# Splitting GpSimd's weight subtraction into pieces of two blocks, in a two-layer transformer kernel

## What is computed

```python
n = rms_norm(h, norm_mix_w[layer])
h = h + token_mixer(n, positions, w_in[layer], ...)
n = rms_norm(h, norm_ffn_w[layer])
h = h + conv_gated_mlp(n, w_ffn_in[layer], ...)
...
x = x + g1 * mix_lat
x = x + g2 * _sq_relu_mlp(_modulate(_rmsnorm(x, norm2_g[layer]), sh2, sc2), w_mlp1[layer], w_mlp2[layer])
```

## Time and profile before

| | before |
|---|---|
| median of three executions | 3695.28 us |
| the profiled execution: its time | 3697.86 us |
| its span, from first to last instruction | 3696.1 us |
| mean granted clock of TensorE | 0.952 |
| TensorE busy | 3334.1 us, 90% |
| VectorE busy | 2352.3 us, 64% |
| ScalarE busy | 1555.8 us, 42% |
| GpSimd busy | 1424.0 us, 39% |

### The profile page before, as it was taken

One profiled execution on the slowest core, in us unless ns is written; L12 is line 12 of the kernel. 1 busy time (PEld: TensorE's weight loads), 2 busy tenths in 40 slices (PEclk: granted clock), 3 DMA queues, 4 the chain that ended last, 5 costly groups with the idle time before them and its releaser, 6 DMA issues.

```text
span 3696.1 us, 58768 instructions
## 1 busy us (share of the span) xinstructions
PE 3334.1 (90%) x21604; PEld 2999.2 (81%) x21604; DVE 2352.3 (64%) x3370; ACT 1555.8 (42%) x2196; POOL 1424.0 (39%) x672
## 2 busy tenths in 40 slices
PE   5898989899989999999987987888887999999998
PEld 4888988898867878878865977888886788888886
DVE  5777777776746873883874766676765653535353
ACT  4344433443334443443434554354443443434343
POOL 2334443444323444444421333444442344444442
PEclk7999999999989999999998998899998999999999
DMA  4655555555565556556543756554564566666653
GB/s 159 203 188 185 192 188 189 179 192 191 173 219 181 182 173 186 182 172 186 175 151 120 252 167 197 190 189 157 182 205 170 190 194 189 186 185 186 188 183 108
DMA packets 262387, 672.95 MB, mean 182 GB/s; under 512 B 28263, under 2 KB 66888, under 8 KB 261448
## 3 DMA queue, kind: packets, MB, share of 16 engines
q1 hardware_dynamic: 262152, 669.81, 56.4%
HBM read 663.38 MB, written 6.32 MB: 181 GB/s over the span
## 4 chain that ended last, share of the span: by engine, by line
PE 56%; DVE 21%; issue 12%; ACT 5%; POOL 3%; DMA 2%; DVEq 1%; SPq 0%; ACTq 0%; POOLq 0%
PE psum L639 21%; PE psum L640 10%; PE psum L632 4%; PE psum L634 4%; PE psum L633 4%; POOL w_lo L497 3%; ACT w_hi L487 2%; PE psum L709 2%; DVE w_lo L497 2%; DVE psum L478 2%; PE psum L637 1%; DVE work L1262 1%; PE psum L1406 1%; DVE work L763 1%; DVE work L1641 1%
## 5 line engine op out<-in xcount | busy, mean ns | idle before, releaser
L497 POOL TENSOR_TENSOR w_lo<-raw,w_hi 128x1024 fp32r<-128x1024 f32 (+3 forms) x668 | 1423.8, 2133 | 2240.6 <-ACT w_hi L487 2239.3
L487 ACT ACTIVATE w_hi<-raw 128x1024 fp32r<-128x1024 f32 (+3 forms) x1112 | 1045.8, 947 | 1353.2 <-PE psum L634 616.7
L632 PE MATMUL psum<-act_a,w_lo 128*128 128x256 f32 x3072 | 923.3, 301 | 32.5 <-DVE w_lo L497 13.6
L497 DVE TENSOR_TENSOR w_lo<-raw,w_hi 128x1024 fp32r<-128x1024 f32 (+3 forms) x444 | 538.9, 1214 | 580.9 <-ACT w_hi L487 572.7
L633 PE MATMUL psum<-act_a,w_hi 128*128 128x256 f32 x3072 | 886.1, 288 | 0.0
L634 PE MATMUL psum<-act_a,w_hi 128*128 128x256 f32 x3072 | 885.4, 288 | 0.0
L639 PE MATMUL psum<-act_a,w_hi 128*128 128x512 f32 x2295 | 828.1, 402 | 26.7 <-DVE act_a L751 10.8
L639 PE MATMUL psum<-act_b,w_hi 128*128 128x512 f32 x2096 | 760.9, 404 | 29.7 <-DVE act_b L1649 17.7
L640 PE MATMUL psum<-act_a,w_lo 128*128 128x256 f32 x2295 | 647.3, 282 | 0.0
L632 PEld LDWEIGHTS psum<-act_a,w_lo 128*128 128x128 f32 x3072 | 608.2, 198 | 42.4 <-issue 18.5
L633 PEld LDWEIGHTS psum<-act_a,w_hi 128*128 128x128 f32 x3072 | 608.1, 198 | 3.1 <-issue 1.9
(11 more groups left out here) (335 smaller groups left out, 3348.4 us busy)
## 6 DMA issues: line engine op xcount, KB each, us to landing
raw<-w_mlp SPq DMA_DIRECT2D x256, 512.0 KB, 4.3
raw<-w_up SPq DMA_DIRECT2D x176, 512.0 KB, 3.7
raw<-w_dil SPq DMA_DIRECT2D x192, 384.0 KB, 3.4
work<-w_ada SPq DMA_DIRECT2D x288, 256.0 KB, 4.0
raw<-w_hg SPq DMA_DIRECT2D x128, 320.0 KB, 3.1
raw<-w_delta SPq DMA_DIRECT2D x64, 512.0 KB, 4.1
raw<-w_out SPq DMA_DIRECT2D x64, 512.0 KB, 5.7
raw<-w_down SPq DMA_DIRECT2D x64, 512.0 KB, 3.8
```

Of the source, the lines that this page charges most:

```text
L487: act.activation(w_hi[:, t % SPLIT, 0:nb * P], raw[:, t % RAW, 0:nb * P], ACT.Copy)\
L497: eng.tensor_tensor(w_lo[:, t % SPLIT, 0:nb * P], raw[:, t % RAW, 0:nb * P], w_hi[:, t % SPLIT, 0:nb * P], ALU.subtract)\
L632: pe.matmul(bank[:, 0:S], wl, src[:, kt, 0:S], start=first, stop=False)
```

## The change

GpSimd makes the low part in pieces of two blocks (256 columns): an item of eight blocks takes four instructions in place of one, an item of six takes three, an item of five takes three (of 256, 256 and 128 columns), an item of two blocks one as before. Only the last piece raises the semaphore, only the first is preceded by the wait, and the pieces stand back to back in GpSimd's stream. VectorE's items stay whole (`step = nb`).

```diff
                 nb = ph.items[t][1]
                 wait(eng, "hi_ready", i * ph.ipb + (ph.g0 + t + 1))
-                eng.tensor_tensor(w_lo[:, t % SPLIT, 0:nb * P], raw[:, t % RAW, 0:nb * P],
-                                  w_hi[:, t % SPLIT, 0:nb * P], ALU.subtract)\
-                   .then_inc(sem(f"lo_ready_{who}"), 1)
+                step = 2 if who == "pool" else nb
+                for b in range(0, nb, step):
+                    cols = slice(b * P, min(b + step, nb) * P)
+                    ins = eng.tensor_tensor(w_lo[:, t % SPLIT, cols], raw[:, t % RAW, cols],
+                                            w_hi[:, t % SPLIT, cols], ALU.subtract)
+                ins.then_inc(sem(f"lo_ready_{who}"), 1)
```

## The result

The changed kernel takes 3607.84 us (median of four, 3598.61 to 3613.75), the kernel before beside it 3696.03 us (median of four). The ratio is 0.976, with a 95% interval of 0.9743 to 0.9777: 88 us faster. The forecast was 3652 us, 43 us faster. The side was right and the time lies in the range, but the gain is twice the size that was forecast.

What follows compares the result with a forecast made beforehand. TensorE was taken to wait mostly for VectorE, held during single GpSimd instructions. Gains 23.5 ("one") + 17.6 + 4 ("two") + 3.6 ("up") + 3 ("out", "ctx"), less 4 and 5, made 43 us: 3695 to 3652 us, range 3605 to 3698.

Steps and rivals of the forecast that it cites:

- Rival 3: VectorE isn't let in between pieces and is held for the whole item: slower, 3726 us; chance 0.06.
- (f): Phase "two", wait at L2082: L2011 and L2012 held for shorter, 2.2 us, eight times, 17.6 us gained.
- (g): Phase "two", scans (L1994) ahead of L2011 and L2012: fewer hits, 0.5 us a body, 4 us gained.
- (a): Phase "one", wait at L1432: L1486 done some 1.2 us sooner, the wait goes, 5.6 us counted.
- (e): Phase "one", wait at L1396: L1310 gains, but L1316 and L1320 give it back; 0.2 us, eight times, 1.6 us.
- (d): Phase "one", wait at L1384: L783 and L785 hit by two subtractions; 0.8 us, eight times, 6.4 us gained.
- rival 2: Shorter waits keep the clock at 2.4 GHz in "two", sometimes "one": some 25 us more, 3627 us; chance 0.08.
- (h): Phase "two", wait at L2212: a train pays every piece once; nothing, between 1 us lost and 1 gained a body.
- (b): Phase "one", wait at L1571: L785 released sooner, 0.6 us, six times, 3.6 us gained.
- (c): Phase "one", wait at L1597: one hit on L1262 shortened, 0.9 us, seven times, 6.3 us gained.
- Rival 1: VectorE operations let in early are followed by others held by further pieces; about 5 us left, 3690 us; chance 0.16.
- Rival 4: GpSimd falls behind in "two": 2 us a body come back, gain in "one" stays, 3675 us; chance 0.05.

Runs made afterwards that it cites:

- long-first kernel: Against the kernel before: GpSimd's items cut into as many instructions as in the change, the long piece first, then pieces of two columns; 3693.86 us, ratio 0.9992.

## Why the prediction was right in kind and wrong in size

**The mechanism** stands. L2011 and L2012 went from 2.29 and 2.28 us to 1.22 and 1.21, where the forecast had them done 2.2 us sooner together; it was 2.1. Rival 3, that VectorE isn't let in between pieces without a wait between them, is out: four pieces ran back to back there. That operations with an operand in PSUM aren't held is borne out too: in the kernel before, no group of VectorE's operations that read PSUM, line by line and shape by shape, has a longest duration over 4% above its median. The Trainium skill (SBUF — State Buffer, section "Who interferes with whom") says that a VectorE instruction with two SBUF inputs and a GpSimd instruction that reads SBUF exclude each other for the whole instruction, whichever starts first; the traces agree, with the old L1641 at up to 2514 ns beside whole items and 846 ns beside pieces of 256 columns, in place of 424, and with GpSimd's long piece at 2.25 us in place of 1.82 where VectorE was first. The Trainium skill's warning (GPSIMD Engine Reference, section 2.1) that one instruction's end doesn't hold back the next was no obstacle to the hand-over.

**Step (f)** was right: L2011 and L2012 give 2.1 us a body, and the wait at L2082 fell by 19.3 us, against 17.6 for (f) and 4 for (g), the scans ahead of it, of which some 2 came. **Step (a)** was right: 6.4 us against 5.6. **Step (e)** was nearly right: the wait at L1396 grew by 1.6 us where a gain of 1.6 was counted. **Step (d)** was too high: 3.2 us at L1384 against 6.4.

**Four steps made the forecast too low.** The first is the largest.

1. *The pairs "up" and "down"*, 3.6 us in the sum, measured 21 us alone. Two things were missed. The waits at the ends of "up" fell by 8.0 us, not 3.6. Before, L1649 alone was held for 2.2, 2.2 and 1.7 us ahead of the three ends, and TensorE's waits fell by 3.0, 3.2 and 1.8 us, so at the first two more than this one hold came off. In the changed kernel VectorE has no work left over there: it pauses for 0.78 us or more before its L688, which it didn't before. And the last "down" gave 11.0 us, for which the sum had no term.
2. *The clock*, nothing in the sum (rival 2 placed some 25 us of it in "two"). TensorE's busy time fell from 3334.1 to 3310.2 us with the same 21604 products, 24 us. But "two" has only 3.2 us of it, and its granted clock stays at 0.90 to 0.91: 4.6 us of the wait at L2082 are left in nearly every body, and in the 2 us behind one of them (2289 to 2291) the clock is 0.50, as before. The most is in the last "down", 7.9 us; out has 3.1, "one" 2.7, and the rest is in smaller parts. The last section says what is known of it.
3. *The losses*, 9 us in the sum: 4 for late low parts, 5 for new hits. Late low parts cost 1.6 us (TensorE's waits for GpSimd went from 12.9 us, of which the forecast had read only the 7.5 at L639, to 14.5), and of TensorE's waits for VectorE the one at L1396 grew by 1.6 us and no other by as much. So some 3 us of the 9 can be seen. New hits that only made a gain smaller can't be told apart in these traces, and the long-first kernel doesn't settle it, since its unchanged time is a sum of gains and losses of about this size.
4. *Trains*, step (h), nothing in the sum, measured 8.0 us (32.4 to 24.4). The forecast let each piece of 0.77 us hold a train for 0.77 us. The traces show the price to be smaller. Before, with whole items:

```profile
2380.87 3.50 DVE L2141 TENSOR_SCALAR work<-work 128x256 f32<-128x256 f32 x3
2384.40 2.59 DVE L2146 SCALAR_TENSOR_TENSOR work<-work 128x255 f32<-128x255 f32 x6
```

After, at the same place:

```profile
2313.50 1.96 DVE L2144 TENSOR_SCALAR work<-work 128x256 f32<-128x256 f32 x3
2315.49 4.16 DVE L2149 SCALAR_TENSOR_TENSOR work<-work 128x255 f32<-128x255 f32 x6
```

The first three win 1.54 us, and the six behind them, none of which was held before, lose 1.57. So the train does take it back, as the forecast said of this place; but from the first line's start to the last one's end it is 6.12 us before and 6.15 after, with nine pieces of GpSimd beside it in place of three whole items, so the added fixed time of GpSimd's costs the train nothing. Five of the nine pieces fall beside the six L2149 and add 1.57 us to them, 0.31 us each: less than a piece's own 0.77. TensorE's wait behind this train is 0.75 us shorter (3.39 before, 2.64 after). The operation ahead of the train gives 0.41 of it (the copy at L2136, 0.88 us before, 0.47 after); where the rest comes from wasn't followed. In "one" steps (b) and (c) were too low, 7.7 us at L1571 against 3.6 and 10.3 at L1597 against 6.3; with (a), (d) and (e) the five waits give 26.0 us against 23.5, and TensorE's shorter busy time the other 2.7 of the 28.6.

Together, by the kernels with one phase changed: 17 us more than forecast in the pairs, with their share of the clock, 7 in "one", 7 in "two", 5 in out, ctx and out2, and the 9 that the sum took off for losses, since what the phases gained is already net of them. These make the 45 that were missing. That the time still lies in the range, 3 us above its lower end, is luck: the range reached so far down for rival 2, the clock in "two", and that is not what happened.

**Rival 1** (trains take it back) is out as the rule, though L1396 and L2141 to L2150 show it at two places. **Rival 4** (GpSimd late in "two") is out for two blocks; with pieces of one block its waits were 27.9 us and still worth it.

## What to carry to other kernels

When an operation on VectorE has the same shape and place each time and its longest duration is several times its median, look at what GpSimd has under way at that moment: the hold shows as a longer duration, not as a wait. What it costs is set by the length of one GpSimd instruction, so cut GpSimd's elementwise work into pieces as short as its slack allows; cutting VectorE's as well gained nothing here. A delay of GpSimd's long instructions by about a microsecond or less gave 32 us in this kernel, whose bodies repeat, so a single timing doesn't prove a cause: vary the length, and put the long piece first. Time taken off VectorE pays only where TensorE waits for it: half of its subtractions in "one" moved away, and it brought nothing.

## What was not expected of the hardware

A wait of TensorE of under 2 us can go with a fall of the clock, but its length doesn't decide it. Before, in the last "down", L1821 is held, TensorE waits 1.83 us and its next four products take 3.53 us:

```profile
1904.42 2.19 DVE L1821 TENSOR_TENSOR work<-work 128x512 f32<-128x512 f32 x1
```

```profile
1906.67 3.53 PE L1893 MATMUL psum<-work 64*128 64x512 f32 x4 [1.83 <-DVE work L1821]
```

After, it is held for one piece, TensorE waits 0.74 us and the same four products take 1.98 us:

```profile
1858.73 1.10 DVE L1824 TENSOR_TENSOR work<-work 128x512 f32<-128x512 f32 x1
```

```profile
1859.89 1.98 PE L1896 MATMUL psum<-work 64*128 64x512 f32 x4 [0.74 <-DVE work L1824]
```

This looks like a cause, but two other kernels speak against it. With pieces in "two" alone, the last "down" has its whole items, the hold and the wait of 1.83 us, and yet the four products take 1.98 us:

```profile
1905.57 1.98 PE L1896 MATMUL psum<-work 64*128 64x512 f32 x4 [1.83 <-DVE work L1824]
```

The long-first kernel shows the same (1.80 us of waiting, then 1.98). And in the kernel that gave GpSimd more of phase one, the wait here is 0.74 us, as in the changed kernel, but the clock falls a few microseconds later. These are the granted clocks of the 15 us that begin with the four products, in the kernel before, in the changed kernel and in that one; they are 0.77, 1.00 and 0.78:

```profile
1906.67:1921.67 15.00, 15.00 (x53) 9.62 (x54) 7.89 (x14) 1.69 (x2) 1.83 (x1) 0.77 0.01 1
```

```profile
1859.89:1874.89 15.00, 14.28 (x58) 8.88 (x59) 8.73 (x14) 1.89 (x3) 4.22 (x5) 1.00 0.01 1
```

```profile
1862.20:1877.20 15.00, 14.24 (x51) 9.09 (x52) 8.76 (x14) 1.92 (x3) 4.25 (x5) 0.78 0.01 1
```

A mean below 1.00 is time at 1.2 GHz in place of 2.4 GHz. What makes the clock fall in one of these kernels and not in another stays open. The length of the last "down" shows the same spread: 139.8 to 142.0 us in four kernels that cut GpSimd's items there into one or two blocks, 144.8 with pieces of four blocks, 148.9 to 152.9 in five profiles with a long instruction there (the kernel before among them), but also 148.9 in the kernel that gave GpSimd more of phase one and 152.2 in the one that cut VectorE's items, both of which have short pieces there. Each of these is one profiled execution. So the clock's share of the 88 us, some 24 us by TensorE's busy time, isn't shown to follow from the shorter holds, and is the least certain part of the gain.
